# A mixture-of-experts layer on one core: the 60 experts behind the first four are taken in an order of their token counts that the chip works out itself

## What is computed

```python
scores = jax.nn.sigmoid((h @ router_w).astype(jnp.float32))
choice = scores + router_bias
...
_, idx = lax.top_k(masked, TOP_K)                      # 8 of 64 experts a token
wts = wts / jnp.sum(wts, axis=-1, keepdims=True) * ROUTE_SCALE
...
xb = h_pad[rt]                                         # rows of the tokens of one expert
hid = jax.nn.silu(xb @ w1[e]) * (xb @ w3[e])           # 1024 -> 256
ob = (hid @ w2[e]) * rw[:, None]                       # 256 -> 1024
return y.at[rt].add(ob.astype(y.dtype)), None
```

## Time and profile before

| | |
|---|---|
| median of 3 runs | 2559.64 us (2558.33 to 2562.93) |
| the profiled execution | span 2559.0 us from first to last instruction |
| the MoE items in it | 1585 to 2544 us on PE, then the last adds up to 2559.0 |
| PE busy | 2430.9 us, 95% of the span |
| DMA share | 0.73 to 0.99 in each 100 us from 1600 to 2500 |

### The profile page before, as it was taken

How to read it: one execution, slowest core, us unless ns; L and a number is a source line. 1 busy time by engine, 2 the same in 40 slices (tenths; PEclk the granted TensorE clock), 3 DMA queues, 4 the chain that set the end, 5 groups by cost and what they waited for, 6 DMA issues and landing times.

```text
span 2559.0 us, 32436 instructions
## 1 busy us (share of the span) xinstructions
PE 2430.9 (95%) x8542; PEld 1183.9 (46%) x8543; DVE 1184.1 (46%) x2728; ACT 483.6 (19%) x892; POOL 641.5 (25%) x653
## 2 busy tenths in 40 slices
PE   6999999999999999999999999999998998998997
PEld 3444444555545565565444553344443443443443
DVE  3466232666645656763355764233333333333332
ACT  3311001444431233332111122000000000000000
POOL 0000000000021000001111535455445445534441
PEclk9999999999999999999999999999999999999999
DMA  8221335342362422223334125788799799989894
GB/s 258 64 52 41 77 84 147 103 136 95 114 163 70 99 59 74 78 95 119 108 111 127 67 89 196 241 288 257 240 315 311 236 307 356 335 263 355 307 298 100
DMA packets 122932, 437.49 MB, mean 171 GB/s; under 512 B 22204, under 2 KB 24460, under 8 KB 97120
## 3 DMA queue, kind: packets, MB, share of 16 engines
q1 hardware_dynamic: 78208, 306.91, 34.6%
q0 software_dynamic: 44640, 129.49, 19.6%
HBM read 369.72 MB, written 73.93 MB: 173 GB/s over the span
## 4 chain that ended last, share of the span: by engine, by line
PE 83%; DVE 7%; another core or an unknown queue 3%; issue 2%; DMA 2%; ACT 1%; SPq 1%; POOL 0%; ACTq 0%; DVEq 0%; POOLq 0%
PE psum L986 21%; PE psum L1466 17%; PE psum L1516 8%; PE psum L1071 8%; PE psum L1317 6%; PE psum L1334 3%; PE psum L1471 3%; PE psum L1274 2%; PE psum L1522 2%; PE psum L1378 2%; PE psum L1142 2%; PE psum L1152 2%; PE psum L1161 1%; PE psum L1401 1%
## 5 line engine op out<-in xcount | busy, mean ns | idle before, releaser
L986 PE MATMUL psum<-mem 128*128 128x512 f32 x1536 | 691.3, 595 | 1.3 <-DMA mem<-in_w_in 1.1
L1466 PE MATMUL psum<-mem 128*128 x1008 | 451.6, 604 | 7.5 <-issue 7.1
L779 POOL DMA_INDIRECT mem<-h_d,idx x312 | 317.5, 1018 | 395.3 <-DVE idx L2716 274.9
L986 PEld LDWEIGHTS psum<-mem 128*128 128x128 f32 x1536 | 279.8, 191 | 295.0 <-issue 291.7
L1466 PEld LDWEIGHTS psum<-mem 128*128 128x128 f32 x1008 | 193.8, 194 | 265.1 <-issue 264.9
L2694 DVE TENSOR_TENSOR mem<-mem,psum 128x256 f32<-128x256 f32 x93 | 39.1, 422 | 491.9 <-ACT mem L1931 448.2
L1516 PE MATMUL psum<-mem 128*128 128x512 f32 x504 | 245.9, 620 | 2.5 <-issue 1.3
L1071 PE MATMUL psum<-mem 128*128 128x512 f32 x448 | 192.8, 592 | 0.0
L784 POOL DMA_INDIRECT out_x<-mem,put x93 | 142.0, 1527 | 134.7 <-issue 86.9
L1931 ACT ACTIVATE mem<-psum 128x256 f32<-128x256 f32 x93 | 35.7, 385 | 720.3 <-PE psum L1466 371.6
L1317 PE MATMUL psum<-mem 128*128 128x512 f32 x384 | 165.0, 592 | 0.0
(11 more groups left out here) (403 smaller groups left out, 2509.5 us busy)
## 6 DMA issues: line engine op xcount, KB each, us to landing
mem<-in_exp_w SPq DMA_DIRECT2D x201, 1024.0 KB
mem<-in_w_in SPq DMA_DIRECT2D x16, 2048.0 KB, 14.2
proj_d<-mem SPq DMA_DIRECT2D x104, 256.0 KB, 2.0
mem<-in_ada_w POOLq DMA_DIRECT2D x16, 1024.0 KB, 6.2
mem<-proj_d POOLq DMA_DIRECT2D x56, 256.0 KB, 2.9
mem<-proj_d POOLq DMA_DIRECT2D x20, 512.0 KB, 5.8
mem<-in_ada_w SPq DMA_DIRECT2D x4, 2048.0 KB, 23.0
mem<-in_w_branch SPq DMA_DIRECT2D x3, 2048.0 KB, 8.1
```

The source lines that it names most:

```text
L779: g.indirect_dma_start(x[:, 2 * P * n:2 * P * (n + 1)], None, h2_q, bass.IndirectOffsetOnAxis(ap=idx[:, p, j, n:n + 1], axis=0), bounds_ch ...
L986: mm = t.matmul(bank(unit_bank(u)), l, r, start=(k == 0), stop=(k == KD - 1))
L1466: return t.matmul(bank(4 + j), xgT[r][:, k, P * j:P * (j + 1)], up_piece(h, r, k), start=(k == 0), stop=(k == KD - 1))
```

## The change

The first four entries of the table stay experts 0 to 3. The 60 entries behind them hold the other experts in an order by token count: largest, smallest, 21st, second largest, second smallest, 22nd, and so on. The rank of each is found on DVE, one expert per partition: a key (count times 64 minus number) is compared with the keys of all 60, the comparisons that it loses are counted, and where `turn_of` (the rank that belongs to each place) equals the rank, `placed` gets the expert's count and number. One more matmul of ones spreads `placed` over all partitions, and `table` copies it into `tab`. The rests of large experts stay at the end. The core of the diff:

```diff
+            t.matmul(psum[:, 7, 256 + 3 * NV:256 + 3 * NV + 2 * NR], ones[0:NE, :], placed.rearrange("p a b -> p (a b)"), start=True, stop=True)
             t.matmul(psum[:, 7, 256:256 + 3 * NV], ones[0:NE, :], items.rearrange("p a b -> p (a b)"), start=True, stop=True).then_inc(s_ts, 1)
...
+            turns, third = turn_of.rearrange("e (k j) -> e k j", j=3), NR // 3
+            v.tensor_copy(turns[:, :, 0:1], col_i[0:NE, 0:third].unsqueeze(2))
+            v.tensor_scalar(turns[:, :, 1:2], col_i[0:NE, 0:third].unsqueeze(2), -1.0, float(NR - 1), ALU.mult, ALU.add)
+            v.tensor_scalar(turns[:, :, 2:3], col_i[0:NE, 0:third].unsqueeze(2), float(third), None, ALU.add)
+            v.tensor_scalar(own_e, tok[0:NE, 0:1], float(FAR), None, ALU.add)
+            link(v.tensor_scalar(is_late, tok[0:NE, 0:1], float(FIXED - FAR), None, ALU.is_ge))
...
-                link(v.tensor_scalar(tab[:, 0, 0:NE], psum[:, 7, 0:NE], float(WIDE), 1.0, ALU.min, ALU.max))
+                link(v.tensor_scalar(tab[:, 0, 0:FIXED], psum[:, 7, 0:FIXED], float(WIDE), 1.0, ALU.min, ALU.max))
...
+                v.scalar_tensor_tensor(out=key_row, in0=psum[0:NE, 7, FIXED:NE], scalar=float(NE), in1=col_i[0:NE, FIXED:NE],
+                                       op0=ALU.mult, op1=ALU.subtract)
+                v.scalar_tensor_tensor(out=own_key, in0=own, scalar=float(NE), in1=own_e, op0=ALU.mult, op1=ALU.subtract)
+                v.tensor_scalar(own_n, own, float(WIDE), 1.0, ALU.min, ALU.max)
...
+            def order_items():
+
+                link(v.tensor_scalar(key_row, key_row, own_key, None, ALU.is_gt))
+                link(v.tensor_reduce(own_rank, key_row, AX.X, ALU.add))
+                link(v.tensor_scalar(picked, turn_of, own_rank, is_late, ALU.is_equal, ALU.mult))
+                link(v.tensor_scalar(placed[:, 0, :], picked, own_n, None, ALU.mult))
+                link(v.tensor_scalar(placed[:, 1, :], picked, own_e, None, ALU.mult))
...
+                sorted_in = psum[:, 7, 256 + 3 * NV:256 + 3 * NV + 2 * NR].rearrange("p (a b) -> p a b", a=2)
+                link(v.tensor_copy(tab[:, 0, FIXED:NE], sorted_in[:, 0, :]))
+                link(v.tensor_copy(tab[:, 1, FIXED:NE], sorted_in[:, 1, :]))
+                link(v.tensor_scalar(tab[:, 2, FIXED:NE], sorted_in[:, 1, :], float(NT), None, ALU.mult))
```

More of the change, by code:

```diff
@@ L224, in layer_kernel @@
         past, over, items = view(12000, NV)[0:NE, :], view(12040, 4)[0:NE, :], view(12048, 3, NV)[0:NE]
+        FIXED = 4
+        NR = NE - FIXED
+        assert NR % 3 == 0
+        turn_of, key_row, picked = (view(11392 + NR * j, NR)[0:NE, :] for j in range(3))
+        placed = view(11392 + 3 * NR, 2, NR)[0:NE]
+        own_e, own_key, own_rank, own_n, is_late = (view(11392 + 5 * NR + j, 1)[0:NE, :] for j in range(5))
         SBLOCKS = ["mqk", "hf", "hq", "g0"]
@@ L2531, in count_items @@
                 link(v.memset(tab[:, 2, NE + NV - 1:NE + NV], 0))
-                link(v.tensor_scalar(tab[:, 2, 0:NE], col_i[:, 0:NE], float(NT), None, ALU.mult))
-                link(v.tensor_copy(tab[:, 1, 0:NE], col_i[:, 0:NE]))
+                link(v.tensor_scalar(tab[:, 2, 0:FIXED], col_i[:, 0:FIXED], float(NT), None, ALU.mult))
+                link(v.tensor_copy(tab[:, 1, 0:FIXED], col_i[:, 0:FIXED]))
                 dve.wait_ge(s_cn, 1)
-                link(v.tensor_scalar(tab[:, 0, 0:NE], psum[:, 7, 0:NE], float(WIDE), 1.0, ALU.min, ALU.max))
+                link(v.tensor_scalar(tab[:, 0, 0:FIXED], psum[:, 7, 0:FIXED], float(WIDE), 1.0, ALU.min, ALU.max))
                 link(v.tensor_scalar(n_col, psum[0:NE, 7, NE:NE + 1], -float(WIDE), None, ALU.add))
+                own = psum[0:NE, 7, NE:NE + 1]
+                v.scalar_tensor_tensor(out=key_row, in0=psum[0:NE, 7, FIXED:NE], scalar=float(NE), in1=col_i[0:NE, FIXED:NE],
+                                       op0=ALU.mult, op1=ALU.subtract)
+                v.scalar_tensor_tensor(out=own_key, in0=own, scalar=float(NE), in1=own_e, op0=ALU.mult, op1=ALU.subtract)
+                v.tensor_scalar(own_n, own, float(WIDE), 1.0, ALU.min, ALU.max)
                 link(v.tensor_scalar(past[:, 0:3], col_i[0:NE, 0:3], float(WIDE), n_col, ALU.mult, ALU.is_lt))
                 v.tensor_reduce(n_over, past[:, 0:3], AX.X, ALU.add).then_inc(s_tp, 1)
+            def order_items():
[4 more added lines that the diff above has]
+                link(v.tensor_scalar(placed[:, 1, :], picked, own_e, None, ALU.mult))
             def list_items():
@@ L2610, in _ @@
             count_items()
+            order_items()
             shared_hidden(5)
```

## The result

The changed kernel takes 2498.63 us (2495.00 to 2499.96, 4 runs) where the kernel before takes 2561.01 (2558.33 to 2562.93, 4 runs): ratio 0.9752, interval 0.9738 to 0.9766, 62 us faster. The forecast was 2495 with a range of 2484 to 2530. The number holds for the chip of these runs.

A forecast was written before the change was run, and what follows sets the result against it. The prediction took PE to be bound by matmuls except for 106 us lost, mostly at half items, to semaphores held by POOL's runs. 2559.0 - 66.8 - 0 + 1 + 1 = 2494 profiled, 2495 as median; range 2484 to 2530.

The forecast's parts named there:

- Half items, -66.8 us: At the 17 half items, with 2 gathers beside each of 16 in groups, PE's loss falls from 70.4 to 3.6 us.
- Behind half items, 0: At the 16 items standing behind half ones, 23.6 us lost against 23.5 before: nothing gained.
- The weak point: Items behind half ones: POOL's 8.9 us run should end with the product up; bounds 0 less, or 2 us more each.
- rival (2): The delay moves to the item behind the half one, 2 to 3 us more in 16 places: 2535; chance 0.1.
- Large items, +1: Large items, beside their successor's 8 gathers and 1 add, lose 0.1 on each of 20: 2 us against 1 before.
- The list, +1: Building the ordered table on DVE and PE ahead of the items costs 0.3 to 0.9 us, taken as 1.
- Item 1, unchanged: Item 1, near the start of the MoE part, keeps its loss of 9.3 us.
- the share of the unknown releaser: Chain time given to a releaser the trace doesn't know, 8.6% of 963 us before, should fall to near 0.
- the 93% and 0.98: Sign: no 100 us window of the middle with PE under 93% or a clock under 0.98.
- Rival (1): Three groups where DMA and PE meet run at 340 GB/s or less: 2500, with neighbouring groups late 2510; chance 0.1.
- Rival (3): The delay belongs to half items themselves; they keep their 70 us, the list costs 1: 2561; chance 0.05.
- its rule: A semaphore of PE that falls into a run of POOL's indirect DMAs can reach ACT only when the run ends.

The follow-up runs named there:

- rotated: Changed kernel with each group of three turned to small, middle, large: 2490.22 us, ratio 0.9980, in a later set 2491.22 us, 0.9979, both on the second chip.
- exchanged: Changed kernel with small and large swapped in every second group: 2576.51 us, ratio 1.0057, on the first chip; 2558.79 us, 1.0003, on the third.
- reversed: Changed kernel with each group in the order large, middle, small: 2491.86 us, ratio 0.9985, on the second chip.
- sorted: Changed kernel with the 60 experts in falling order of tokens: 2532.82 us, ratio 0.9885; with half of the up weights left out 2499.90 us, 1.0014, on the second chip.

## Why the prediction was right, and what it didn't know

**Half items, -66.8 us.** Measured -67.3 (70.4 to 3.1). Right in place and size; 15 of the 16 in groups lose at most 0.1, item 50 1.7, item 66 2.0. The prediction took each of the 16 to have the next half item's 2 gathers beside it, which item 50 hasn't: it is the last half item of the groups, so what stands three places on has 65 tokens. Its run of 4 gathers and an add begins with its product up (2264.79 and 2264.4) and lasts till 2271.56.

**Behind half items, 0.** 23.6 was forecast for the 16 places, 21.1 measured (23.5 before). The weak point held, and rival (2) with it fell: the silu at 1940.00 behind item 23 starts when the product up ends. These 21 us are the price that stays on either chip (21.2 on the second).

**Large items, +1.** Others lose 4.7 where 3 was forecast and 1 stood before. It is the term that was sized too small, by some 2 us, and it's 4.9 on the second chip, so it isn't the delay.

**The list, +1.** With the old order it is 0.9996 (0.9987 to 1.0005) of the time before; in the changed kernel PE comes to item 0 at 1583.5 us (1585.3 before), on the second chip at 1585.8 (1585.3).

**Item 1, unchanged.** 10.4 for 9.3. It is the longest piece of the chain that the trace can't name, so the share of the unknown releaser didn't go near 0 as said but to 2.8% of 901 us:

```profile
1594.38 16.76 another core or an unknown queue
2263.87 8.30 another core or an unknown queue
```

The first is item 1, under the long run of gathers at the start; the second, item 50. The window 1600 to 1700, with 92.4 and a clock of 0.97, holds item 1's stall, and is the one that misses the 93% and 0.98 that the prediction named.

**Weights.** They keep up at a share of 1.01 and 350 GB/s, without one wait for `in_exp_w`. Rival (1) asked for 340 GB/s or less in the three tight groups; they stand from 2177 to 2286 us, and the rate there is 350, so neither its condition nor its price came.

**The end.** Not in the prediction: the last add is issued about 6 us behind the last matmul's end in both kernels, but from that end to the span's end it is 19.1 us (2477.8 to 2496.9) where it was 14.7 (2544.3 to 2559.0), 4.4 more. Every kernel with the old order has 14.7 to 15.0 us there, the changed and rotated ones 18.3 to 19.1, the other orders 15.9 to 16.9. This is why 66.5 us at the last matmul are 62.1 in the span. The traces show where it goes. The last add has landed 10.5 us behind PE's end in the kernel before and 10.9 in the changed one, and what follows is one instruction, POOL's closing DRAIN. It takes 3.96 us in each kernel with the old order, 7.92 and 7.83 in the changed and rotated ones, 5.18 in the exchanged and 5.79 to 5.83 in the reversed and sorted ones, and where an order ran on more than one chip it was the same there. As to luck, the item terms add up to 39.4 us lost where 40 was forecast, with misses of -2.5 and +1.7 that nearly cancel, and the 3.6 us by which 2498.6 is over 2495 are about what the DRAIN adds. Why the order changes it is open; no run was aimed at it.

**Rival (3), and what was wrong in the reasoning.** The delay doesn't belong to half items as such: the exchanged order has it with the same items on two chips, and item 1, of class one, has it too. But the prediction took its rule for one of the kernel, and left 0.05 for its absence. The rule holds on two of the three chips. The records of the semaphores can be counted, with care, since on the chips with the delay many are missing: 6844 of all engines from 1585 us on in the kernel before, where the second chip has 10816. So a late record is often only the next one. PE's turn of item 23 in the changed kernel ends at 1931.38 and has no record before 1941.42, yet ACT copies its result at 1931.42. Counting only those of PE's increments whose record comes over 3 us behind the matmul's end with no other increment of that semaphore in between, there are 12 in the kernel before and 5 in the changed one, 36 and 27 in the exchanged order on the first and third chips, and none in either kernel on the second. Whether the taking of records has a part in the delay, no run here shows.

**A rule stated too broadly.** The records also show that the rule was too broad on a chip that has the delay. Take as a run POOL's indirect DMAs with pauses under 0.7 us. In the kernel before on the first chip, 53 of PE's increments with over 2 us of a run still ahead are recorded at once, and 17 over 0.3 us late (22 have no record of their own). How old the run is tells them apart: in its first 4 us 47 come at once and 2 late, behind that 6 and 15. In the exchanged order on that chip it is 39 and 9, and behind the 4 us 3 and 28. On the second chip all 119 of the kernel before come at once. So a run of 2 gathers and an add is over about when the delay would set in, and a run that begins with a half item's product up is 4 us old when that ends. No run was made to test this.

**What the number owed to the chip.** The Trainium skill's page TensorE: Matmul & The Clock Gate (section The cost: per-tile semaphore tail) gives a matmul's semaphore some tens of ns by its formula. The second chip agrees, with 0.04 us at item 25; the first doesn't, with 9.8 us at the same item (1972.65 to 1982.48). Had the changed kernel been timed on the second chip first, its 2489 would have been inside the range all the same, by luck, against a kernel before of 2496, and the gain would have been 0.27% instead of 2.5%.

## What to carry to other kernels

Before an order of work is tuned around a stall, profile the kernel on a second chip: a stall that isn't there is no property of the kernel, and a gain made of it comes only where the stall is. Where items of very different compute and equal bytes pass through one queue, alternate them; it was worth 6.5 us of 2496 on the chip without the delay, and it also lets each item's helper traffic stand beside an item that can cover it. A run that is postponed by a wait isn't shortened, so look first at which item it falls on next. And a full queue doesn't say which bytes a stretch waits for: look at what PE waits for, and follow the chain.

## What the runs showed of the hardware

On the first and the third chip an increment of PE's semaphores that falls into a run of POOL's indirect DMAs, and mostly one over 4 us old, can come up to 11 us late; on the second none does (the counts are above). On the first chip the long run of gathers at the start holds up more than PE's semaphores. The run is the same on the first and second chip, an instruction each 1.30 us from 1589.9 on. From the chain of the kernel before within it, on the first chip:

```profile
1599.85 0.71 issue
1600.56 0.70 DVEq L2756
1602.71 0.71 issue
1603.42 0.70 DVEq L438
```

The branch of line 2756 takes DVE's sequencer 0.70 us there and 0.07 on the second chip (at 1597.96), inside the same run. Such steps are few: inside runs of three and more indirect DMAs 4% of DVE's sequencer steps are over 0.5 us long on the first chip, and the median is 0.06 us there and 0.05 on the second. A gather takes POOL 1018 and 1015 ns, so POOL itself isn't slower. Two increments of PE made 8 matmuls apart, at 1786.62 and 1788.33 us (beside item 12 of the kernel before), are recorded at 1794.13 and 1794.22, 0.3 and 0.4 us behind the end of POOL's run at 1793.86. That two delays of different length end together looks like increments that are held, not slow ones. What holds them, and what differs between the chips, no run here shows.
